# Order of the attention units and of the loads ahead of them in a fused hybrid layer

## The reference

```
h = modulate(rmsnorm(x), shift1, scale1)          # 6 modulation vectors: silu(c) @ ada_w
mq,mk,mv,mo,mi,mf, sz,sxbc,sdt, nq,nk,nv = split(h @ w_in)
m_out = bidirectional mLSTM(mq, mk, mv, ...)      # 4 heads
s_out = bidirectional SSD scan(sxbc, sdt, ...)    # 6 heads, then * silu(sz), rmsnorm
context: a_out = softmax(nq nk^T / 8) nv          # 6 heads, 128 x 128
latent:  row r, 16 query columns: 8 rows x 32 columns of keys around them
         p = softmax([q k_loc^T / 8 + rpb bias (masked), q k_cache^T / 8])
         a_out = p_loc v_loc + p_cache v_cache    # 6 heads
x = x + gate1 * ([m_out | s_out | a_out] @ w_out)
x = x + gate2 * moe(modulate(rmsnorm(x), shift2, scale2))   # 16 experts, expert choice
y = rmsnorm(x)
```

## Time and profile before

| | |
|---|---|
| time, median of 3 runs | 1768.84 us (1768.38 to 1770.77) |
| the profiled execution's own time | 1773.37 us |
| its span | 1771.6 us |
| PE busy | 1660.1 us (94%) |
| DVE, ACT, POOL busy | 728.9, 392.8, 428.4 us |
| granted PE clock, mean | 0.971 |
| the attention, first scores to first output product | 601.82 to 738.41 us |

### The profile page before, as it was taken

One profiled execution on the slowest core, in us unless ns is written; L12 is line 12 of the kernel. 1 busy time (PEld: TensorE's weight loads), 2 busy tenths in 40 slices (PEclk: granted clock), 3 DMA queues, 4 the chain that ended last, 5 costly groups with the idle time before them and its releaser, 6 DMA issues. The chain is left out here.

```text
span 1771.6 us, 29473 instructions
## 1 busy us (share of the span) xinstructions
PE 1660.1 (94%) x11668; PEld 1450.1 (82%) x11668; DVE 728.9 (41%) x1833; ACT 392.8 (22%) x948; POOL 428.4 (24%) x504
## 2 busy tenths in 40 slices
PE   5999999979999779999989999999999999999991
PEld 3876877756568656788879999999999999999991
DVE  4001056666445847422364332444433324444333
ACT  5220113331212546411121111111111111111112
POOL 2000000025223623111113223332322233322223
PEclk9999999989999889999989999999999999999996
DMA  8411100021102467532279888888888888888836
GB/s 318 127 36 57 31 26 24 25 78 41 37 28 81 86 216 209 169 107 76 79 263 353 295 275 265 297 267 282 299 281 291 274 259 296 266 293 298 276 85 239
DMA packets 205823, 323.52 MB, mean 183 GB/s; under 512 B 30112, under 2 KB 93465, under 8 KB 205755
## 3 DMA queue, kind: packets, MB, share of 16 engines
q1 hardware_dynamic: 181307, 284.23, 46.3%
q0 software_dynamic: 10160, 19.62, 5.6%
q10 hardware_dynamic: 14288, 18.76, 3.2%
HBM read 291.82 MB, written 27.55 MB: 180 GB/s over the span
## 5 line engine op out<-in xcount | busy, mean ns | idle before, releaser
L1751 PE MATMUL psum<-arena 128*128 128x144 f32 x4096 | 506.4, 287 | 3.3 <-DVE arena L2320 2.4
L1751 PEld LDWEIGHTS psum<-arena 128*128 128x128 f32 x4096 | 504.3, 190 | 4.0 <-DVEq L2328 2.5
L823 POOL DMA_INDIRECT expert_list<-gt x136 | 151.9, 1117 | 454.2 <-DVE gt L2351 381.0
L1766 PE MATMUL psum<-arena 128*128 128x144 f32 x2048 | 255.2, 287 | 0.0
L1766 PEld LDWEIGHTS psum<-arena 128*128 128x128 f32 x2048 | 251.7, 190 | 0.4
L1348 PE MATMUL psum<-arena 128*128 128x384 f32 x720 | 246.3, 498 | 0.1
L2366 DVE TENSOR_TENSOR arena<-gt,psum 128x144 f32<-128x144 f32 x128 | 39.0, 305 | 420.7 <-PE psum L1751 390.6
L1348 PEld LDWEIGHTS psum<-arena 128*128 128x128 f32 x720 | 135.9, 193 | 93.0 <-issue 7.0
L2232 DVE SCALAR_TENSOR_TENSOR arena<-arena,gt 128x1024 f32<-128x1024 f32 x136 | 168.9, 1279 | 0.0
L1351 PE MATMUL psum<-arena 128*128 128x256 f32 (+2 forms) x864 | 165.7, 353 | 0.0
L1351 PEld LDWEIGHTS psum<-arena 128*128 128x128 f32 x864 | 146.2, 192 | 18.0 <-issue 1.7
(11 more groups left out here) (344 smaller groups left out, 1757.8 us busy)
## 6 DMA issues: line engine op xcount, KB each, us to landing
arena<-in_exp_w SPq DMA_DIRECT2D x96, 2048.0 KB, 9.6
arena<-in_ada_w SPq DMA_DIRECT2D x24, 1024.0 KB, 6.6
arena<-in_w_in SPq DMA_DIRECT2D x11, 1024.0 KB, 5.2
arena<-affinity_rows SPq DMA_DIRECT2D x17, 512.0 KB
arena<-in_x_sample SPq DMA_DIRECT2D x16, 512.0 KB, 4.8
arena<-decay_rows ACTq DMA_DIRECT2D x24, 192.0 KB, 3.3
out<-arena SPq DMA_DIRECT2D x9, 512.0 KB
arena<-in_w_out SPq DMA_DIRECT2D x4, 1024.0 KB, 5.2
```

Of the source, the lines that this page charges most:

```text
L823: pool.indirect_dma_start(out=list_d, out_offset=bass.IndirectOffsetOnAxis(ap=rank_i[:, c:c + 1].bitcast(U32), axis=0), in_=pair[:, c, :], ...
L1751: ins = mm(bank[:, 0:SLOTS], w[:, k, col], xeT[:, k, :], start=(k == 0), stop=(k == KD - 1))
L1766: ins = mm(bk[4 + db % 2][:, 0:SLOTS], wslot[4 + db // 4][:, k, (db % 4) * P:(db % 4) * P + P], hid[:, k, :], start=(k == 0), stop=(k == K ...
```

## The change

The order of the units: the three context units now come first (units 0 to 2), then the latent ones, pair by pair (3 to 10, 11 to 18, 19 to 26). `MOD_UNITS` is a new list, so slabs 8 and 9 are multiplied behind units 1 and 2, and none behind the last three. The two late SSD tiles move behind units 3 and 4 (`LATE_UNITS`).

SP's list: the source of the first table gets memory of its own (two places that are free earlier), so its two halves are loaded during the SSD scan. Then slabs 8 and 9, the value blocks of pair 0, slabs 10 to 13, and only then what pair 1 needs. So that slabs 8 and 9 fall into ring slots 0 and 1, whose last readers are the last projections, and not into 2 and 3, two empty places stand in the list of slabs, and the ring's count is corrected for them (`loads_of_slot`). POOL makes table 0 ahead of the other masks. PE's first score products wait only for what their accumulators need; DVE takes the first two units' maxima ahead of the last SSD statistics.

```diff
-    return [ada[m] for m in MODS1] + win1 + win2 + ada[8:] + wout
+    return [ada[m] for m in MODS1] + win1 + win2 + [None, None] + ada[8:] + wout
-    G1, WOUT = 22, 38
+    G1, WOUT = 24, 40
-        rel = view(R_HT + 2304, 2, 2, 2 * HR * KW)
+        rel = [[Cst.rearrange("p a b c d -> p (a b c d)")[:, 0:2 * HR * KW], view(R_S + 6020, 2 * HR * KW)]] +             [[view(R_HT + 2304 + (2 * hp + e) * 2 * HR * KW, 2 * HR * KW) for e in range(2)] for hp in range(2)]
+        for s in (G1 - 2, G1 - 1):
+            last_read[s] = (yz, NT)
-        MOD_UNITS = [3, 4, 6, 7, 9, 10, 12, 13, 15, 16, 18, 19, 21, 22, 24, 25]
-        AU = [(hp, t) for hp in range(HN // 2) for t in range(-1, NL)]
+        MOD_UNITS = [1, 2, 5, 6, 8, 9, 11, 12, 13, 14, 17, 18, 19, 20, 22, 23]
+        AU = [(hp, -1) for hp in range(HN // 2)] + [(hp, t) for hp in range(HN // 2) for t in range(NL)]
+        LATE_UNITS = [3, 4]
...
-            sp.wait_ge(pj_full, pe_index[n_proj - 1] + 1)
-            for hp in range(2):
-                load_rel(hp)
-            sp.wait_ge(pj_act, evacuated("A", n_proj))
-            sp.wait_ge(yz, NT)
-            for hp in range(2):
-                load_values(hp)
-            for m in range(8, 18):
+            sp.wait_ge(out_done, 16 * 18)
+            load_rel(0, 0)
+            sp.wait_ge(sU, NU - 2)
+            load_rel(0, 1)
+            for m in range(8, 10):
+                load_slab(G1 + m - 8)
+            sp.wait_ge(pj_act, evacuated("A", n_proj))
+            sp.wait_ge(sJ, NU)
+            load_values(0)
+            for m in range(10, 14):
+                load_slab(G1 + m - 8)
             sp.wait_ge(pj_full, pe_index[n_proj - 1] + 1)
+            for e in range(2):
+                load_rel(1, e)
+            sp.wait_ge(sY, NU)
+            load_values(1)
+            for m in range(14, 18):
                 load_slab(G1 + m - 8)
-            sp.wait_ge(tab_done, 6)
-            load_rel(2)
-            for m in range(18, 20):
-                load_slab(G1 + m - 8)
+            for e in range(2):
+                load_rel(2, e)
             sp.wait_ge(aO, done_with_pair(0))
             load_values(2)
-            for m in range(20, 24):
+            for m in range(18, 24):
                 load_slab(G1 + m - 8)
...
POOL
-            make_mask(0, 1)
-            make_mask(0, 2)
             for i in range(2):
                 pool.memset(tab[:, i, :, 384:512], 0.0)
+            make_table(0)
             for k in done_at[17]:
                 y_rstd(k)
-            for i in range(2):
-                make_table(i)
+            make_mask(0, 1)
+            make_table(1)
+            make_mask(0, 2)
PE
+            pe.wait_ge(sP, 2 * NU)
+            pe.wait_ge(sH, NU)
+            a_scores(0)
+            pe.wait_ge(sT, NU)
+            pe.wait_ge(pj_act, evacuated("A", len(groups)))
+            a_scores(1)
             pe.wait_ge(cache_in, 32)
             pe.wait_ge(sY, NU)
-            pe.wait_ge(pj_act, evacuated("A", len(groups)))
-            a_scores(0)
-            a_scores(1)
-            y_late(0)
...
-                if a == 0:
-                    y_late(1)
+                if a in LATE_UNITS:
+                    y_late(LATE_UNITS.index(a))
DVE
-            for k in done_at[17]:
-                y_mean(k)
...
             a_bias(0)
+            a_bias(1)
             for k in done_at[17]:
-                y_scale(k)
-            a_bias(1)
+                y_mean(k)
...
+                if a == 1:
+                    for k in done_at[17]:
+                        y_scale(k)
```

More of the change, by code:

```diff
@@ L418, in hybrid_layer, with loads_of_slot @@
                 last_read[g[1]] = (pj_full, pe_index[n] + 1)
+        for s in (G1 - 2, G1 - 1):
+            last_read[s] = (yz, NT)
+        def loads_of_slot(s):
+            return s // RING + (0 if s >= G1 and s % RING in ((G1 - 2) % RING, (G1 - 1) % RING) else 1)
         def pj_bank(q):
@@ L471, in done_with_pair @@
         def done_with_pair(hp):
-            return 9 * (hp + 1)
+            return HN // 2 + NL * (hp + 1)
         @block.sync
@@ L507, in _ @@
                     sp.dma_start(Hst[half_g, 2 + d, g, :], state_sT[d, half_g, :]).then_inc(state_in, 16)
-            for s in range(8 + RING, G1):
+            for s in range(8 + RING, G1 - 2):
                 load_slab(s)
@@ L516, in _, with load_rel @@
                 sp.dma_start(new_m[d].rearrange("(a b) -> a b", a=1), gate(MN, d)[0:1, 0, :]).then_inc(out_done, 16)
[L520 to L527, removed]
+            def load_rel(hp, e):
+                for r in range(HR):
+                    first = rpb_pad[192 + (2 * hp + e) * 465 + 31 * (r - 4) - QC:][0:1]
+                    src = bass.AP(tensor=first.tensor, offset=first.offset, ap=[[1, QC], [31, 2 * HR], [1, KW]])
+                    dst = rel[hp][e][QC * r:QC * r + QC, :].rearrange("p (a b) -> p a b", b=KW)
+                    sp.dma_start(dst, src).then_inc(rel_in[hp % 2], 16)
             def load_values(hp):
@@ L769, in make_table @@
                 for e in range(2):
-                    w = rel[:, hp % 2, e, :].rearrange("p (a b) -> p a b", b=KW)[:, r0:r0 + 12, k0:k0 + 2 * QC]
+                    w = rel[hp][e].rearrange("p (a b) -> p a b", b=KW)[:, r0:r0 + 12, k0:k0 + 2 * QC]
                     ins = pool.tensor_tensor(tab[:, i % 2, e, 0:384].rearrange("p (t c) -> p t c", c=2 * QC),
@@ L1256, in slab_ready @@
             def slab_ready(s):
-                pe.wait_ge(slab_in[s % RING], 16 * (s // RING + 1))
+                pe.wait_ge(slab_in[s % RING], 16 * loads_of_slot(s))
             def mods(ms, slab0, between=lambda m: None):
@@ L1513, in y_late @@
                 pe.wait_ge(s_y, NT - LATE + n + 1)
+                pe.wait_ge(modT_done, 8 + sum(w < LATE_UNITS[n] for w in MOD_UNITS))
                 if n >= 1:
@@ L1572, in late_product @@
                 pe.wait_ge(modT_done, m)
-                pe.wait_ge(s_rows_a, LATE)
+                pe.wait_ge(s_rows_a, sum(w < MOD_UNITS[m - 8] for w in LATE_UNITS))
                 if m == 12:
```

## The result

The changed kernel takes 1754.65 us (median of 4 runs, 1753.04 to 1755.06), the one before 1768.61 us (4 runs, 1765.80 to 1770.77): a ratio of 0.992, 95% interval 0.9903 to 0.9937. Timed once more later it took 1752.98 us against 1767.45 us, 0.9912 (0.9895 to 0.9928). The forecast was 1753.1 us, with 1748 to 1759 as its range.

What follows compares the result with a forecast made beforehand. PE, 94% busy, bounds the kernel; the attention has 26.8 us idle plus half clock. First output product: 616.5 + 12.6 + 84.7 + 6.3 + 2.6 = 722.7 against 738.41, so 1768.8 - 15.7 = 1753.1 us, range 1748 to 1759.

Steps and rivals of the forecast that it cites:

- The transfers: SP's list: earlier issue removes PE's waits of 4.46 and 8.45 us; SP's new waits cost nothing, tightest spare 7 us.
- The opening: PE's first units, three context units first: idle 3 and 1.3 us, partly half clock, scores of unit 5 at 616.5 us.
- The steady units: Loops 6 to 24 on PE: 84.7 us at earlier per-unit prices (4.84, 4.86, 3.56), 4 us either way allowed.
- The time: After the first output product PE has no gap, so all 15.7 us reach the end: 1753.1 us.
- The rule on the clock: PE's opening: full clock does not engage for transposes, so the lower level would stay until near unit 5.
- rival 1: Opening slower than its parts: half clock until loop 5, all divisions contended; about 5 us lost, 1758.5 us, chance 12%.
- The upper bound of 5 us: Opening with every step at half clock, contended divisions, no overlap: scores 5 near 622, +5.5 us on the sum.
- The rule on the shared port: DVE's divisions beside POOL's tables: exclusive port adds some 1.3 us to a latent unit's chain in loops 3 and 4.
- Rivals 2, 3 and 4: Values' wait moves (1761, 5%); 1.8 us issues delay slabs (about 1773, 4%); late DVE/POOL step holds units (1766 to 1769, 3%).

## Why the prediction was right

| step | predicted | measured after |
|---|---|---|
| first slab issued | 593.2, the release of before | 589.75 |
| values of pair 0 issued | 597.1 to 608.0 | 596.61 to 607.07 |
| pair 1's small transfers end | 635.5 | 636.70 |
| slab 18 issued | 668 | 668.39 |
| scores of unit 2 | 604.6, idle 3 | 604.62, idle 3.45 |
| product of slab 8 ends | 611.4 | 611.3 |
| product of slab 9 waits | 1.3 | 1.51 |
| scores of unit 5 | 616.5 | 616.09 |
| unit 5 to the first output product | 106.2 | 105.99 |
| first output product | 722.7 | 722.08 |

**The transfers.** Both waits for them went, and SP's new waits cost nothing, as priced. One release was put too late, without effect: slab 8 went at 589.75 us, right behind the table sources, and not at 593.2, where SP had been released before. The experiments sharpen the step: the transfers alone shorten the stage by 16.24 us in one profile and by 14.30 in another. The prediction priced the whole schedule and did not say that in the stage the order of the units is nearly replaceable, nor that the early products of slabs 8 and 9 are what keeps SP's stand-still cheap (in the kernel with the transfers alone, where they come later, it cost 1.48 us at PE).

**The opening.** Scores at 1.65 us and the slab at 1.94 us, both prices from rows of before, came back to the hundredth. The gap itself was half a us longer than summed (5.53 us from the scan's last transposes to the scores of unit 2, against 5.0), and unit 5 came 17.00 us behind those transposes where 16.9 were summed: smaller errors of the other sign in between, which is luck. The clock was full from about 611 on: the four scores at 611.25 take 0.92 us.

**The steady units.** With product and pick a unit took 4.84 us (691.29 to 696.13), with pick only 3.56 (669.21 to 672.77): the numbers of the earlier trace rows. This is why these units gave an error of 0.2 us and not the 4 allowed.

**The time.** The stage shrank by 15.83 us, and 15.7 were forecast; the medians went down by 14.0 in one timing and 14.5 in the other. The prediction carried the whole gain to the end because what follows has no gap; those rows cover only 750 to 800 us. Ahead of 835.64 us of the profile of before PE stands for 2.31 us, and runs at half clock behind it for a time that differs between executions. The missing 1.4 to 1.8 us are within what the parts outside the stage vary; which part they come from is not shown.

**The rule on the clock** (rival 1, the Trainium skill's TensorE: Matmul & The Clock Gate, Part 4) says that the full clock does not engage for transposes. It did not hold this opening down: transposes stand at 605.51, 608.76 and 613.15 with scores, values and a slab's product between them, and the clock went from 0.50 to 1.00 among them. No run here has a long stream of transposes. The upper bound of 5 us was not needed.

**The rule on the shared port** (the Trainium skill's SBUF — State Buffer, section SBUF: two separate sides) says that GpSimd and a vector instruction in a 2-port mode exclude each other; the trace agrees in that DVE's divisions take nearly three times as long beside POOL, and whether one waits wholly for the other it does not show. DVE's division of a latent unit and POOL's tables:

```profile
618.69 2.46 DVE L2164 TENSOR_SCALAR gt<-gt,arena 128x512 f32<-128x512 f32 x2
...
631.44 0.88 DVE L2164 TENSOR_SCALAR gt<-gt,arena 128x512 f32<-128x512 f32 x2
```

```profile
618.73 1.00 POOL L784 TENSOR_TENSOR arena<-Cst,arena 128x384 f32<-128x384 f32 x1 [0.80 <-DVE arena L2152]
```

The pair that stands beside table operations takes 2.46 us, the later one, with POOL still, 0.88. Loops 3 to 5 took 12.74 us (616.09 to 628.83) where 12.6 were summed, so the price was covered.

**Rivals 2, 3 and 4.** Value transfers land 2.0 to 3.0 us after issue, so those of pair 0 were there by about 610 us, wanted at 621.48. A value transfer took 10.46/16 = 0.65 and 10.78/16 = 0.67 us to issue, not 1.8. And no late step on DVE or POOL held the first latent units: behind the 1.51 us that the sum had, PE waits 0.90 and 0.79 us there.

## What to carry to other kernels

Look first at the one queue that issues the transfers: here 64 small ones at 0.5 to 0.7 us each stood ahead of a 1 MB load. Moving them shortened the stage by 14.3 to 16.2 us, where the whole change gave 15.8, and gave about 10 of its 14 us in the time, while reordering the computing against the old queue left the time where it was (0.9992). A queue that waits for a product passes the delay on to all that stands behind it, and it can come back to PE through two or three other engines: follow the wait back before you call it an engine's. A schedule of waits can be added up to within a us over 123 from neighbouring rows of the trace, if a long gap is charged twice: once as itself, once as the slow work behind it. And where short independent work is left, as the slab products here, put it behind the units whose copy would otherwise stand bare, to the very end of the loop.

## What the runs showed of the hardware

The half clock behind a gap of 3.45 us in the opening cost 2.42 us more, taken away by filling the gap with unread products; a gain at one wait can be given back at the next (2.6 us ahead at unit 5, 0.3 at the end, behind a wait of 1.79 us). The length of a wait alone does not say whether the clock falls. The same program kept 1.00 behind a wait of 1.48 us in one profile and had 0.50 behind 1.39 us at the same place in another, and did both behind the same 1.71 us; behind the same 2.31 us, six us of gapless work ran at a mean of 0.76 in one profile and 0.59 in another. A stage read from one profile can therefore be off by about 2 us (122.58 and 124.52 for the same kernel).

Settled in part only is why the kernel with the early transfers alone is 3.6 to 5.4 us slower in the median than the kernel after. In the one profile near its median 1.6 us lie in the stage and 2.4 in the stretch behind it, where the half clock lasts longer; that this holds in its other executions, and why it should in this kernel more than in the other, is not shown.
